# A two-stream decoder layer in fp32: squares and scalings placed by the build-time order, next x summed on VectorE, leader's x loaded first

## The reference, cut to what matters

```python
D_MODEL = 1024; D_FF = 2816; PLE_DIM = 256; EPS = 1e-6
def rms_norm(x, g):
    return x * lax.rsqrt(jnp.mean(x * x, axis=-1, keepdims=True) + EPS) * g
def swiglu(x, w_gate, w_up, w_down):
    return (jax.nn.silu(x @ w_gate) * (x @ w_up)) @ w_down
def decoder_layer(x, p, ...):
    h = x + 0.5 * rms_norm(swiglu(rms_norm(x, ng[0]), f1_gate, f1_up, f1_down), ng[1])
    mix, s_new, conv_new = token_mixer(rms_norm(h, ng[2]), ...)   # GLA heads + gated conv of 3 taps
    h = h + rms_norm(mix, ng[3])
    h = h + 0.5 * rms_norm(swiglu(rms_norm(h, ng[4]), f2_gate, f2_up, f2_down), ng[5])
    gate = jax.nn.sigmoid(rms_norm(h, ng[6]) @ w_ple_gate)
    h = h + rms_norm((p @ w_ple_proj) * gate, ng[7])
    return h, s_new, conv_new
```

## Time and profile before

| what | value |
|---|---|
| runs of the kernel before | 1646.17 us median of 3 (1643.25, 1646.17, 1696.57) |
| the profiled execution | 1645.65 us; span of its slowest core (core 1) 1644.0 us |
| outside the span | 1.65 us |
| spans of the eight cores | 1631.0 to 1644.0 us |
| matmul busy | 1537.0 us, 93% of the span |
| ScalarE, VectorE, GpSimd busy | 736.5, 715.9, 268.5 us |
| DMA | 305.39 MB, mean 186 GB/s |

### The profile page before, as it was taken

How to read it: one execution, slowest core, us unless ns; L and a number is a source line. 1 busy time by engine, 2 the same in 40 slices (tenths; PEclk the granted TensorE clock), 3 DMA queues, 4 the chain that set the end, 5 groups by cost and what they waited for, 6 DMA issues and landing times.

```text
span 1644.0 us, 27962 instructions; the slowest of 8 cores (1631.0 to 1644.0 us)
## 1 busy us (share of the span) xinstructions
PE 1537.0 (93%) x9454; PEld 1492.4 (91%) x9454; DVE 715.9 (44%) x1421; ACT 736.5 (45%) x1437; POOL 268.5 (16%) x512
## 2 busy tenths in 40 slices
PE   6999999899998999999989999799998998999996
PEld 5999889889997999989989999799998997889995
DVE  3331464543324643155554422573315754433136
ACT  3112665642147611275574124841138474511266
POOL 3211210112121221111112112022111110111110
PEclk9999999999998999998999999899999995999998
DMA  9865843468666796565446668399556443566661
GB/s 282 255 186 160 233 142 102 112 181 250 186 193 191 208 328 209 170 184 167 102 156 208 200 176 249 112 279 319 177 160 202 137 142 100 158 177 175 203 190 69
DMA packets 83452, 305.39 MB, mean 186 GB/s; under 512 B 9538, under 2 KB 12498, under 8 KB 82548
## 3 DMA queue, kind: packets, MB, share of 16 engines
q0 software_dynamic: 73040, 283.97, 58.4%
q1 hardware_dynamic: 10276, 19.65, 3.7%
HBM read 292.83 MB, written 10.75 MB: 185 GB/s over the span
## 4 chain that ended last, share of the span: by engine, by line
PE 79%; DMA 7%; ACT 6%; DVE 4%; issue 4%; DVEq 0%; SPq 0%; ACTq 0%; POOLq 0%; POOL 0%
PE ps_bank L472 78%; DMA sb_wring<-f2a 3%; DMA sb_wring<-f2b 2%; ACT L519 2%; DMA sb_wring<-f1b 1%; ACT sb_xnB L519 1%; DVE sb_hB L522 1%; DVE sb_xnB L522 1%; DMA sb_ngl<-ngl 1%; ACT sb_ta L519 1%; PE ps_bank L496 1%; ACT sb_WA L519 1%; PE ps_bank L504 0%; ACT sb_sqB L519 0%; DVE sb_WA L527 0%
## 5 line engine op out<-in xcount | busy, mean ns | idle before, releaser
L472 PE MATMUL ps_bank<-sb_xnA,sb_wring 128*128 128x344 f32 x2208 | 410.6, 332 | 19.0 <-DVE sb_WA L527 8.6
L472 PE MATMUL ps_bank<-sb_xnB,sb_wring 128*128 128x344 f32 x2208 | 396.6, 323 | 6.6 <-ACT sb_xnB L519 5.7
L472 PEld LDWEIGHTS ps_bank<-sb_xnA,sb_wring 128*128 128x128 f32 x2208 | 370.1, 197 | 27.2 <-issue 26.0
L472 PEld LDWEIGHTS ps_bank<-sb_xnB,sb_wring 128*128 128x128 f32 x2208 | 358.2, 190 | 13.5 <-issue 13.1
L472 PE MATMUL ps_bank<-sb_WA,sb_wring 128*128 128x344 f32 x1872 | 330.7, 323 | 11.4 <-DVE sb_WA L527 4.7
L472 PE MATMUL ps_bank<-sb_WB,sb_wring 128*128 128x344 f32 (+1 forms) x1904 | 333.7, 320 | 1.7 <-DVE sb_wring L522 1.0
L472 PEld LDWEIGHTS ps_bank<-sb_WA,sb_wring 128*128 128x128 f32 x1872 | 301.6, 189 | 17.8 <-issue 17.5
L472 PEld LDWEIGHTS ps_bank<-sb_WB,sb_wring 128*128 128x128 f32 x1904 | 309.1, 190 | 2.6 <-issue 2.4
L607 POOL DMA_DIRECT2D sb_wring<-f2a x132 | 69.7, 528 | 367.1 <-PE ps_bank L472 334.9
L519 ACT ACT_TABLE_LOAD x91 | 116.8, 1283 | 27.4 <-DMA sb_ngl<-ngl 14.4
L607 POOL DMA_DIRECT2D sb_wring<-f1a x132 | 69.7, 535 | 290.7 <-PE ps_bank L472 280.7
(11 more groups left out here) (198 smaller groups left out, 1647.6 us busy)
## 6 DMA issues: line engine op xcount, KB each, us to landing
sb_wring<-f1a POOLq DMA_DIRECT2D x132, 512.0 KB, 10.0
sb_wring<-f2a POOLq DMA_DIRECT2D x132, 512.0 KB, 5.5
sb_wring<-f1b POOLq DMA_DIRECT2D x48, 704.0 KB, 5.5
sb_wring<-f2b POOLq DMA_DIRECT2D x48, 704.0 KB, 5.3
sb_wring<-wca POOLq DMA_DIRECT2D x24, 512.0 KB, 6.8
sb_wring<-wo POOLq DMA_DIRECT2D x24, 512.0 KB, 5.6
sb_wring<-wpg POOLq DMA_DIRECT2D x24, 512.0 KB, 7.3
sb_wring<-wg POOLq DMA_DIRECT2D x12, 512.0 KB, 6.7
```

The source lines that it names most:

```text
L472: ins = e.matmul(out.ap, a.ap, b.ap, start=(first and i == 0), stop=(last and i == n_ - 1))
```

## The change

1. `sqr` and `scl` are new: an operation with two ways, ScalarE (Square, Identity) or VectorE (tensor_tensor, tensor_scalar); the build-time order takes one. They stand for the squares and scalings of `boundary`, `enter` and `xprep`, the square of `out` in `ple`, the scaling in `evac` and the first tap in `conv_tail`. The squares in `evac` stay on ScalarE.
2. The next x: squares are summed on VectorE in two running sums, and two matmuls end it; `bx` is taken only then.
3. Any Exp with scale -0.5 has 20 more priority (`PAIR`).
4. The loads of x over 400 words wide count on the link of the model.
5. The pending operations (the gains `ngl` and stream A's x) are emitted before the other loads of the start.

```diff
+PAIR = 20.0
@@ Prog.op
+        ways = [(eng, fn, kw)]
+        if "other" in kw:
+            ways = [(eng, fn, {"dur": kw.get("dur")}), kw["other"]]
+        new = Op(ways, reads, writes, self.prio)
@@ Prog.settle
-                self.emit_pending(o)
+                self.emit_pending(o, min(range(len(o.ways)), key=lambda w: self.free[o.ways[w][0]]))
@@ Prog.pick
-                o.due = self.ready(o.eng, o.reads, o.writes)
...
+                o.due = [self.ready(w[0], o.reads, o.writes) for w in o.ways]
+            for way, (eng, fn, kw) in enumerate(o.ways):
+                due, free = o.due[way], self.free[eng]
+                t = max(due, free)
...
+                late = max(0.0, t - min(max(d, self.free[w[0]]) for d, w in zip(o.due, o.ways)))
+                key = (t + turn if due > free + 0.15 else free, due - o.prio + turn + late)
@@ Prog.emit_op
+            elif writes and ndma == 1 and width > 400:
+                self.link = max(self.link, start + 2.0) + 0.0018 * width
+                self.done[tok] = self.link + 0.5
@@ act
+            if func == AF.Exp and scale == -0.5:
+                P.prio += PAIR
@@ new helpers
+        def sqr(out, in_):
+            P.op("act", lambda e: e.activation(out=out.ap, in_=in_.ap, func=AF.Square), reads=[in_], writes=[out],
+                 other=("dve", lambda e: e.tensor_tensor(out=out.ap, in0=in_.ap, in1=in_.ap, op=ALU.mult), {}))
+        def scl(out, in_, g):
+            P.op("act", lambda e: e.activation(out=out.ap, in_=in_.ap, func=AF.Identity, scale=g.ap), reads=[in_, g], writes=[out],
+                 other=("dve", lambda e: e.tensor_scalar(out=out.ap, in0=in_.ap, scalar1=g.ap, scalar2=None, op0=ALU.mult), {"dur": 0.4}))
@@ boundary
-                act(q, hp, AF.Square)
+                sqr(q, hp)
                 for k in range(2):
-                    act(xv(S, c + k, n), hv(S, c + k, n), AF.Identity, scale=gvec(gpre, c + k))
+                    scl(xv(S, c + k, n), hv(S, c + k, n), gvec(gpre, c + k))
@@ evac
             act(q, bank.v(0, n), AF.Square)
-            act(raw(S, m, n), bank.v(0, n), AF.Identity, scale=gvec(g, m, half))
+            scl(raw(S, m, n), bank.v(0, n), gvec(g, m, half))
@@ conv_tail
-            act(y1.v(0, npr), u.v(0, npr), AF.Identity, scale=w0)
+            scl(y1.v(0, npr), u.v(0, npr), w0)
@@ enter
-                act(xv(S, c, n), hv(S, c, n), AF.Identity, scale=gvec(0, c))
+                scl(xv(S, c, n), hv(S, c, n), gvec(0, c))
                 q = nsq(S, n)
-                tt(q, hv(S, c, n), hv(S, c, n), ALU.mult)
+                sqr(q, hv(S, c, n))
@@ ple
-            if N is not None:
-                bx = yield from hold()
...
             def xprep(c):
                 xr = S.W.v((10 + c) * n, (11 + c) * n)
-                q = S.W.v((18 + c % 4) * n, (19 + c % 4) * n, r=True)
-                act(q, xr, AF.Square)
-                ts(S.W.v((10 + c) * n, (11 + c) * n, r=True), xr, gvec(0, c), None, ALU.mult, None)
-                xq.append(q)
+                k = 18 + c if c < 2 else 20 + c % 2
+                sqr(S.W.v(k * n, (k + 1) * n, r=True), xr)
+                scl(S.W.v((10 + c) * n, (11 + c) * n, r=True), xr, gvec(0, c))
+                if c % 2 and c > 1:
+                    acc = S.W.v(18 * n, 20 * n)
+                    tt(S.W.v(18 * n, 20 * n, r=True), acc, S.W.v(20 * n, 22 * n), ALU.add)
...
-                    sqr = nsq(S, n)
-                    act(sqr, omr(False), AF.Square)
-                    pend.append(sqr)
+                    q2 = nsq(S, n)
+                    sqr(q2, omr(False))
+                    pend.append(q2)
...
+            xq = [S.W.v((18 + k) * n, (19 + k) * n, r=True) for k in range(2)]
+            bx = yield from hold()
             yield pe(xq, [bx.v(0, n)], True)
-            xsum(0)
+            mm(bx.v(0, n), [(csr.v(C_OD, C_OD + 128, r=True), q) for q in xq])
@@ the start
         for c in range(0, 8, 2):
             load_h(streams[0], tiles[0], c)
+        P.settle(list(P.pending))
```

More of the change, by code:

```diff
@@ L58, with __init__ @@
 class Op:
-    __slots__ = ("eng", "fn", "reads", "writes", "kw", "before", "after", "prio", "due")
-    def __init__(self, eng, fn, reads, writes, kw, prio):
-        self.eng, self.fn, self.reads, self.writes, self.kw, self.prio = eng, fn, reads, writes, kw, prio
+    __slots__ = ("ways", "reads", "writes", "before", "after", "prio", "due")
+    def __init__(self, ways, reads, writes, prio):
+        self.ways, self.reads, self.writes, self.prio = ways, reads, writes, prio
         self.before, self.after, self.due = set(), [], None
@@ L182, in emit_pending @@
             a.before.discard(o)
-        self.emit_op(o.eng, o.fn, o.reads, o.writes, **o.kw)
+        eng, fn, kw = o.ways[way]
+        self.emit_op(eng, fn, o.reads, o.writes, **kw)
     def pick(self):
@@ L190, in pick @@
             if o.due is None:
-                o.due = self.ready(o.eng, o.reads, o.writes)
-            t = max(o.due, self.free[o.eng])
-            tab = o.kw.get("table")
-            turn = SWITCH if tab is not None and tab != self.table else 0.0
-            key = (t + turn if o.due > self.free[o.eng] + 0.15 else self.free[o.eng], o.due - o.prio + turn)
-            if best is None or key < best[0]:
-                best = (key, t, o)
+                o.due = [self.ready(w[0], o.reads, o.writes) for w in o.ways]
+            for way, (eng, fn, kw) in enumerate(o.ways):
+                due, free = o.due[way], self.free[eng]
+                t = max(due, free)
+                tab = kw.get("table")
+                turn = SWITCH if tab is not None and tab != self.table else 0.0
+                late = max(0.0, t - min(max(d, self.free[w[0]]) for d, w in zip(o.due, o.ways)))
+                key = (t + turn if due > free + 0.15 else free, due - o.prio + turn + late)
+                if best is None or key < best[0]:
+                    best = (key, t, o, way)
         return best
@@ L1428, in build_program @@
             if soon is not None and soon[1] <= now + LOOK:
-                P.emit_pending(soon[2])
+                P.emit_pending(soon[2], soon[3])
                 continue
```

13 lines of the change are left out of this document (4 added, 9 removed).

## The result

The kernel after takes 1659.32 us (median of 4 runs, 1657.74 to 1660.14) against 1645.45 for the kernel before (median of 4), a ratio of 1.0082 with a 95% interval of 1.0063 to 1.0100. One of the four runs of the kernel before (1696.57) and some runs of the experiments fell in a slower state of the chip; no ratio here uses them. The kernel after is slower, by less than 2%. The forecast was 1621, the range 1600 to 1643.

A forecast was written before the change was run, and what follows sets the result against it. TensorE was taken as the bound, busy 1537.0 of 1644.0 us; terms -5, -3.9, -10, -8, +1, -1 sum to -26.9, with 2 taken back for overlap -25, giving 1621 us, own range 1611 to 1632, full range 1600 to 1643.

The forecast's parts named there:

- (d): Stage boundaries: VectorE takes scalings after its eight operations, shortening each of B's nine by 0.9 us; -8 us, bounds +9 and -18.
- (e): Evac's scalings out of PSUM on VectorE: 0.51 us each where the plan reckons 0.40; +1 us, bounds 0 and +8.
- (a): Start: loading gains, A's x, then B's x moves both chains forward by 5 us; -5 us, bounds -1 and -9.
- Rival C: B's boundaries: VectorE becomes the late engine, 2.0 us queued ahead of the first addition on each of nine; 1655 us, chance 0.10.
- (c): Two hand-overs between pairs of tiles: a third of 29.2 us idle and lost clock regained; -10 us, bounds 0 and -29.
- rival A: Hand-overs mended almost wholly by the freed bank, worth 27 us instead of 10; 1604 us, chance 0.22.
- (b): Sums of the next x: 24 matmuls fewer at 163 ns each; -3.9 us, bounds 0 and -3.9.
- (f): Priority of Exp: no scaling goes between A's Ln and its Exp; -1 us, bounds 0 and -3.
- Rival D: Weight loads: VectorE scalings from SBUF hold up GpSimd's work by 7 us; 1628 us, chance 0.03.
- Rival B: Whole kernel: ScalarE's relief stays hidden behind other waits, only (a) and (b) are left; 1637 us, chance 0.20.
- shorter waits on B's squares: Sign for (d): B's statistic matmuls wait less on squares, with ScalarE's total down 80 to 150 us and VectorE's up likewise.

The follow-up runs named there:

- e1_bound: Kernel after with the squares and scalings of the boundaries back on ScalarE, all else kept; 0.9911 of the kernel before.
- e9_rank: Kernel after with 12 us added to the rank of every VectorE way among operations VectorE could start at once; 0.9937 of the kernel before.
- e7_bonly: Kernel before with only the squares and scalings of the boundaries free to go to ScalarE or VectorE; 1.0034 of the kernel before.
- both: Kernel after with the squares and scalings of the boundaries and the scaling in evac all back on ScalarE; 0.9855 of the kernel before.
- next x only: Kernel before with only the next x's squares summed on VectorE and the bank bx taken at the end; 0.9892 of the kernel before.
- e5_price: Kernel after with the build-time order reckoning a scaling out of PSUM on VectorE at 0.58 us instead of 0.40; 1.0067 of the kernel before.
- e3_start: Kernel after without the early emission of A's x, so SyncE loads B's x, the gains, A's x as before; 1.0171 of the kernel before.
- g_gate: Kernel after with boundaries and evac on ScalarE, the third weight load waiting for A's x instead of B's; 0.9901 of the kernel before.

## Why the prediction was wrong, point by point

**(d) The boundaries: the step that failed.** I had -8 us and B's nine boundaries 0.9 us shorter each. They became 1.1 us longer to the last scaling and 2.1 us to the last addition. What I wrote was "once VectorE is through with its eight operations it takes scalings"; nothing in the change makes it wait for that. In `pick` an operation that has two ways goes to whichever engine is free first, and then with the high priority that a boundary gives its first pairs, so a square or a scaling of pair 0 passes ahead of the additions of pairs 1 to 3, for which ScalarE and TensorE wait. Reading the key of `pick` with the priorities `URGE + 8 - c` would have shown it. e1_bound and e9_rank take nearly all of that work off VectorE, and the last addition is back at 7.23 and 7.06 us; in e7_bonly it is at 9.42, and the kernel is 0.3% slower where I had 8 us of gain. That it is the order of the queue, and not the amount of work in it, is read from the timeline and the key: no run keeps the amount and changes the order. With evac's scalings, (d) and (e) together are a swing from 0.9855 to 1.0082, some 37 us, where they had -8 and +1. The other four terms had -19.9, and "both", which keeps them, measured -24 (0.9855); with (a) giving nothing and luck of up to 0.8% in any order, that nearness is partly luck. At B's boundaries to the mixer the granted clock is lower as well (0.71 and 0.72 on tiles 3 and 5, 0.89 and 0.90 before), which the prediction had priced only in the hand-overs; how much of the loss is due to that stays open.

**Rival C** is the one that came true in kind: VectorE late at B's boundaries, 1655 by its working against 1659. Its place was wrong. I had put the queue ahead of the first addition, 2.0 us; the first addition is as early as before, and the 2.1 us stand between the additions. That its 1655 lies near the 1659 is luck, since it also counts 5 us for (a) that did not come. I gave it 0.10 and argued against it that "additions have the higher priority"; they have not, the square of the same pair has the same one. That sentence should have been a check of the code.

**(c) The hand-overs** were sized right: -10 forecast, 4.1 and 6.5 us in the two stretches. That is not rival A: TensorE still idles 7.72 and 8.12 us in the two windows, 15.8 in all where it was 17.5, and the lost clock went from 11.7 to 5.4 us. Which cause I had left open is settled in part: the bank and the sum, with hardly any relief of ScalarE, give 1.4 and 5.3 us there in "next x only", and "both" gives 5.4 and 9.2, so the relief of ScalarE adds to it. The edit of the next x alone is worth some 15 us, where (b) and (c) had 13.9 together.

**(a) The start** was -5 and is within 1 us. Both chains moved, but less: the third weight was issued at 19.06, not 17, and its product came at 24.64. I had left out that the wait for B's x now empties the queues: 6 GB/s in the slice at 19 us. The slices at 11 to 17 us carried 2.56 MB, so the bandwidth was used; then nothing was queued.

**(e) Evac** was +1 and costs more: 1.0% when the boundary is free as well, 0.9% when VectorE's ways are ranked last, and 0.6%, inside the intervals, when the boundary is on ScalarE. The price of one scaling was sized at 0.51 us and is 0.576, the upper of my two bounds. The Trainium skill ("VectorE: DVE Perf Modes", Why PSUM operands drop a tier) says that a PSUM operand in fp32 gets no faster mode, and the trace agrees: 0.576 beside 0.392 from SBUF; but I had made that the pace of the two-tensor operation, and it is slower. But e5_price shows that the price matters little. What I missed is the place: 113 operations of 0.58 us, 65 us, on the engine whose additions the boundary waits for. Also the bank is now read by two engines one after the other: both reads together take a median of 1.21 us for A where they took 0.90, worked out from the timelines. That this second point costs anything was argued only, no run takes it alone.

**(f)** ScalarE's table loads fell from 91 to 71; I had counted -1 us for the priority. It was not tried alone. The link of the model I had put at 0, since it does no work on the chip. By my reading of e3_start and g_gate that holds only while both streams' x are emitted ahead of the weights; there one stream's first products came at 46.40 us, 29 and 26 us later than the same stream's in the kernel before. The link was not tried alone.

**Rival D**, the weight loads held up by scalings, is not seen: GpSimd's loads of `f2a` have 528 ns each as before, and land in a median of 5.5 us as before. On the eight cores 27 of them run beside a scaling from SBUF, for 0.37 us on average, and take 546 ns.

**Rival B**, the relief hidden, stood for 1637. It had no term that could make the kernel slower, so it did not come true either.

ScalarE's and VectorE's totals moved by 128 and 126 us, as forecast (80 to 150), but the sign that went with it, shorter waits on B's squares, did not come: 13.4 us became 31.2. That the totals came out right and the time wrong is the lesson of this case.

## What to carry to other kernels

Before giving an engine optional work in a stretch that is bound by latency, ask what stands behind that work on its queue: the balance of the busy times says nothing about it. Optional work belongs behind all work that others wait for. Here that left almost none of it at the boundaries: one term in the ranking turned this change from 0.8% slower to 0.6% faster, mostly by giving the work back to ScalarE, and no version that keeps some of it on VectorE there is measurably faster than the one that keeps none (0.9849 and 0.9855). And where a program's order is made by a greedy search, measure the same edit under two or three neighbouring orders before believing a difference smaller than what a meaningless change makes, here 0.8%.

## What the runs showed of the hardware that was not expected

A tensor_scalar with fp32 output takes 0.576 us for 128x344 out of PSUM and 0.392 from SBUF; the two-tensor operation out of PSUM, which in the groups by form of the same kernel has 0.515, is faster than the one-tensor one. A stop of the weight queues at the start shows only in fine slices: 112, 6 and 127 GB/s in three consecutive microseconds, with 268 and 311 on either side. And equal idling came with very different clocks: in 20 us from the Exp of the same boundary TensorE was busy for 15.07 us at a granted clock of 0.66 in the kernel after, and for 14.43 us at 0.94 in the kernel before, 63 matmuls against 83. By the idle time alone (4.93 and 5.57 us) the kernel after would be ahead there; the lost clock is at most (1 - 0.66) x 20 = 6.8 us, against 1.2.
